# Streaming encoder layer: frame tiles ahead of weights in the first loads, u products by tile as weight blocks arrive, the streams' u later, the last four tiles in halves

## What is computed

```python
h = rms_norm(x, norm_g)
proj = einsum('btd,de->bte', h, w_in)              # 1024 -> 2560
u, g_pool, v_a, v_b, g_conv = split(proj)          # 512 each
pooled = multiscale_pool(u_ext)                    # trailing mean over 2,4,8,16 frames, minus the frame
pooled = (pooled per group @ pool_mix) * pool_scale
pool_out = silu(g_pool) * pooled
v = v_a * sigmoid(v_b)
c = silu(layer_norm(causal_dwconv(v_ext, dw_w, dw_b)))   # 31 taps
conv_out = silu(g_conv) * (c @ pw_w + pw_b)
y = x + concat(pool_out, conv_out) @ w_out
out = rms_norm(y, final_g)
```

## Time and profile before

| what | value |
|---|---|
| runs of the kernel | 282.57, 283.54, 283.54 us, median 283.54 |
| the profiled execution, its time | 284.08 us |
| its span, first to last instruction, slowest core (core 3) | 282.7 us |
| spans of cores 0 to 7 | 280.7, 282.3, 281.2, 282.7, 278.7, 281.8, 278.8, 280.4 us |
| busy share, PE / DVE / ACT / POOL, core 3 | 91% / 64% / 54% / 21% |
| chain that ended last, by engine | PE 64%, ACT 13%, DVE 11%, issue 5%, POOL 3%, DMA 2% |

### The profile page before, as it was taken

One profiled execution on the slowest core, in us unless ns is written; L12 is line 12 of the kernel. 1 busy time (PEld: TensorE's weight loads), 2 busy tenths in 40 slices (PEclk: granted clock), 3 DMA queues, 4 the chain that ended last, 5 costly groups with the idle time before them and its releaser, 6 DMA issues.

```text
span 282.7 us, 4638 instructions; the slowest of 8 cores (278.7 to 282.7 us)
## 1 busy us (share of the span) xinstructions
PE 257.5 (91%) x1768; PEld 140.0 (50%) x1768; DVE 180.0 (64%) x287; ACT 151.8 (54%) x267; POOL 60.2 (21%) x105
## 2 busy tenths in 40 slices
PE   3376999899899999999999899999999999999980
PEld 1175557657444454444566554545444544454430
DVE  1434244455499999999953595357573874767592
ACT  1343734988832459752299726825716634261453
POOL 0129543534500000007100002102202211121232
PEclk9999989999999899999999999999999999999998
DMA  6999999400799463529399029131435532635324
GB/s 132 310 336 340 327 286 332 129 1 2 85 200 193 148 102 95 92 78 205 70 167 165 5 40 326 27 131 74 150 104 196 212 130 106 215 111 211 151 112 184
DMA packets 22952, 44.37 MB, mean 157 GB/s; under 512 B 9649, under 2 KB 13361, under 8 KB 22802
## 3 DMA queue, kind: packets, MB, share of 16 engines
q1 hardware_dynamic: 21154, 38.90, 45.0%
q0 software_dynamic: 1488, 4.85, 11.0%
q10 hardware_dynamic: 288, 0.33, 0.3%
HBM read 38.00 MB, written 10.93 MB: 173 GB/s over the span
## 4 chain that ended last, share of the span: by engine, by line
PE 64%; ACT 13%; DVE 11%; issue 5%; POOL 3%; DMA 2%; SPq 0%; DVEq 0%; ACTq 0%
PE PS L377 59%; PE PS L381 5%; ACT WT L359 5%; DVE PL L373 3%; ACT HG L428 3%; DMA XA<-xp 2%; DVE HG L373 2%; DVE XR L362 2%; POOL STAT L362 2%; ACT HT L359 2%; DVE PA L362 2%; ACT JUNKB L428 1%; DVE XF L362 1%; ACT LNOT L359 1%; POOL STAT L366 1%
## 5 line engine op out<-in xcount | busy, mean ns | idle before, releaser
L377 PE MATMUL PS<-HT,WIN 128*128 128x512 bf16 (+1 forms) x832 | 149.9, 338 | 4.1 <-ACT HT L359 3.1
L377 PEld LDWEIGHTS PS<-HT,WIN 128*128 128x128 bf16 x832 | 72.3, 101 | 69.5 <-issue 6.5
L366 POOL TENSOR_SCALAR STAT<-STAT 128x1 f32<-128x1 f32 (+2 forms) x34 | 14.1, 414 | 112.9 <-ACT JUNKB L428 71.9
L373 DVE SCALAR_TENSOR_TENSOR HG<-XA,STAT,GB 128x1024 bf16<-128x1024 f32 x16 | 21.9, 1371 | 24.9 <-POOL STAT L362 20.6
L428 ACT ACTIVATE JUNKB<-XR 128x1024 bf16<-128x1024 f32 x13 | 13.8, 1058 | 44.6 <-DVE XR L362 44.6
L359 ACT ACTIVATE WT<-WTAB,PP 128x384 bf16<-128x384 f32 x64 | 33.6, 606 | 0.0
L362 DVE TENSOR_TENSOR XR<-PS,XR 128x512 f32<-128x512 f32 x32 | 22.0, 688 | 17.8 <-PE PS L377 17.8
L377 PE MATMUL PS<-WOUT,PL 128*128 128x512 bf16 x128 | 32.9, 379 | 0.0
L377 PE MATMUL PS<-WOUT,MIXC 128*128 128x512 bf16 x128 | 32.9, 379 | 0.0
L359 ACT ACTIVATE HT<-PS 128x1024 bf16<-128x1024 bf16 x16 | 16.4, 1024 | 17.9 <-PE PS L381 17.7
L377 PEld LDWEIGHTS PS<-WOUT,MIXC 128*128 128x128 bf16 x128 | 12.5, 98 | 15.1
(11 more groups left out here) (107 smaller groups left out, 275.4 us busy)
## 6 DMA issues: line engine op xcount, KB each, us to landing
XA<-xp SPq DMA_DIRECT2D x16, 512.0 KB, 16.0
XR<-xp SPq DMA_DIRECT2D x16, 512.0 KB, 3.6
yp<-XR SPq DMA_DIRECT2D x13, 512.0 KB, 2.8
STG<-w_in SPq DMA_DIRECT2D x12, 512.0 KB, 15.8
vdram<-VST SPq DMA_DIRECT2D x4, 520.0 KB, 5.4
VS<-vdram SPq DMA_DIRECT2D x4, 520.0 KB, 5.8
WIN<-w_in POOLq DMA_DIRECT2D x2, 1024.0 KB, 15.9
WOUT<-w_out POOLq DMA_DIRECT2D x1, 2048.0 KB, 20.2
```

Source lines behind the costliest of these rows:

```text
L366: S.op(eng, lambda e: e.tensor_scalar(out=out, in0=a, scalar1=s1, scalar2=None, op0=op0), reads=reads, writes=writes)
L373: S.op('dve', lambda e: e.scalar_tensor_tensor(out=out, in0=a, scalar=s, in1=b, op0=op0, op1=op1), reads=reads, writes=writes)
L377: S.op('pe', lambda e: e.matmul(out, lhsT=lhsT, rhs=rhs, start=start, stop=stop), reads=reads, writes=writes)
```

## The change

1. First loads. On SP's queue the order of the first 512 KB transfers was x0, w8, w9, x1, w10, w11, x2, x3 (x: tile, w: weight block); it is now x0, x1, w8, w9, x2, w10, x3, w11. All later loads keep their order.
2. The first quarter's u. `pre(1)` stands ahead of `trans(0)`, and `utile` is called in smaller pieces: a block of columns for a tile as soon as block and tile can be there.
3. `v_unit(0, 1)` and `v_unit(0, 2)` each move ahead: the second ahead of `pre(4)`, the third ahead of `trans(4)`.
4. `u_h()` moves from ahead of `pre(14)` to behind `trans(15)`; the three weight loads that POOL issues move behind `pre(15)`.
5. `last_tiles()` takes tiles 12 to 15 instead of 13 to 15. One half of a tile's scaling at a time now stands right behind the next square on ACT; tile 14 is stored in two halves as 15 is. `fin_pend` for tile 11 moves behind the second half of tile 12.

```diff
@@ last_tiles
-            for i, p in enumerate(range(NPH - 3, NPH)):
+            for i, p in enumerate(range(NPH - 4, NPH)):
...
-                    if i == 0 and hf == 0:
+                    if pend_scale:
+                        pend_scale.pop(0)()
+                    if i == 0 and hf == 1:
                         fin_pend()
                     tt(XF[i][:, sl], xr[:, sl], FGB[:, sl], ALU.mult, [pk, 'FGB'], [fk])
                     if hf == 0:
                         ts(STAT[:, sc:sc + 1], STAT[:, sc:sc + 1], EPS_RMS, ALU.add, [ssk], [ssk], eng='pool')
-                        if pend_scale:
-                            pend_scale.pop()()
...
-                def scale(i=i, p=p, rs=rs, rsk=rsk):
-                    for hf in range(2):
...
+                def scale(hf, i=i, p=p, rs=rs, rsk=rsk):
...
+                    if p >= NPH - 2:
+                        S.op('act' if p == NPH - 1 and hf == 0 else 'sp',
+                             lambda e: e.dma_start(out=yp_d[p][:, sl], in_=XF[i][:, sl]),
...
-                pend_scale.append(scale)
-            pend_scale.pop()()
+                pend_scale += [lambda f=scale: f(0), lambda f=scale: f(1)]
+            while pend_scale:
+                pend_scale.pop(0)()
@@ first loads
         load_x(0)
         load(ID32[:], id_d, 'ID32', 'c_id', 'act')
+        load_x(1)
         stage_win(8, 'sp')
         stage_win(9, 'sp')
-        load_x(1)
+        load_x(2)
         stage_win(10, 'sp')
+        load_x(3)
         stage_win(11, 'sp')
-        load_x(2)
-        load_x(3)
@@ first quarter
         pre(0)
         cast_win(8, 'dve')
+        pre(1)
+        trans(0)
         cast_win(9, 'dve')
-        trans(0)
-        pre(1)
-        utile(0, (0, 1))
         cast_win(10, 'dve')
+        utile(0, (0,))
+        trans(1)
+        utile(0, (1,))
+        utile(1, (0, 1))
+        pre(2)
+        utile(0, (2,))
+        utile(1, (2,))
         cast_win(11, 'dve')
-        trans(1)
-        utile(0, (2, 3))
-        utile(1)
-        pre(2)
         pre(3)
         trans(2)
+        utile(0, (3,))
+        utile(1, (3,))
+        utile(2, (0, 1))
         trans(3)
-        utile(2)
+        utile(2, (2, 3))
         utile(3)
@@ v units
         v_unit(0, 0)
+        v_unit(0, 1)
         pre(4)
         pre(5)
         cast_win(3, 'pool')
         cast_win(7, 'pool')
-        v_unit(0, 1)
+        v_unit(0, 2)
         trans(4)
-        v_unit(0, 2)
         trans(5)
@@ middle: out of the place ahead of pre(14)
-        S.op('pool', lambda e: e.dma_start(out=PMW[:], in_=pmw_d), writes=['PMW'], dma='wpm')
-        load_win(12, 16, 'wgp')
-        load_win(16, 20, 'wgc')
-        u_h()
...
         pre(15)
+        S.op('pool', lambda e: e.dma_start(out=PMW[:], in_=pmw_d), writes=['PMW'], dma='wpm')
+        load_win(12, 16, 'wgp')
+        load_win(16, 20, 'wgc')
...
         trans(15)
+        u_h()
         pool_sample()
```

More of the change, by code:

```diff
@@ L807, in last_tiles @@
                 tt(rs, STAT[:, sc:sc + 1], NEGH[:, 0:1], ALU.pow, ['SSL%d' % sc, 'NEGH', 'STAT'], [rsk], eng='pool')
-                def scale(i=i, p=p, rs=rs, rsk=rsk):
-                    for hf in range(2):
-                        sl = slice(hf * 512, hf * 512 + 512)
-                        fk = 'XF%d_%d' % (i, hf)
-                        if p == NPH - 1 and hf == 1:
-                            ts(XF[i][:, sl], XF[i][:, sl], rs, ALU.mult, [fk, rsk], [fk])
-                        else:
-                            act(XF[i][:, sl], XF[i][:, sl], AF.Copy, [fk, rsk], [fk], scale=rs)
-                        if p == NPH - 1:
-                            S.op('sp' if hf else 'act', lambda e, sl=sl: e.dma_start(out=yp_d[p][:, sl], in_=XF[i][:, sl]),
-                                 reads=[fk], writes=['o_yp%d_%d' % (p, hf)], dma='stl%d' % hf)
-                    if p < NPH - 1:
+                def scale(hf, i=i, p=p, rs=rs, rsk=rsk):
+                    sl = slice(hf * 512, hf * 512 + 512)
+                    fk = 'XF%d_%d' % (i, hf)
+                    if p == NPH - 1 and hf == 1:
+                        ts(XF[i][:, sl], XF[i][:, sl], rs, ALU.mult, [fk, rsk], [fk])
+                    else:
+                        act(XF[i][:, sl], XF[i][:, sl], AF.Copy, [fk, rsk], [fk], scale=rs)
+                    if p >= NPH - 2:
+                        S.op('act' if p == NPH - 1 and hf == 0 else 'sp',
+                             lambda e: e.dma_start(out=yp_d[p][:, sl], in_=XF[i][:, sl]),
+                             reads=[fk], writes=['o_yp%d_%d' % (p, hf)], dma='stl%d%d' % (p % 2, hf))
+                    elif hf == 1:
                         S.op('sp', lambda e: e.dma_start(out=yp_d[p], in_=XF[i][:]), reads=['XF%d_0' % i, 'XF%d_1' % i],
                              writes=['o_yp%d' % p], dma='st%d' % (p % 6))
-                pend_scale.append(scale)
-            pend_scale.pop()()
+                pend_scale += [lambda f=scale: f(0), lambda f=scale: f(1)]
+            while pend_scale:
+                pend_scale.pop(0)()
         def fin2(p, rs, rsk):
@@ L867, in build_program @@
         JUNKB = at(0, "JUNKB", (128, 1024), BF16)[0]
-        XF = [at(16384 + 4096 * i, "XF%d" % i, (128, 1024), F32)[0] for i in range(3)]
+        XF = [at(16384 + 4096 * i, "XF%d" % i, (128, 1024), F32)[0] for i in range(4)]
         S.op('pool', lambda e: e.memset(NEGH[:], -0.5), writes=['NEGH'])
@@ L1083, in build_program @@
                 p = 4 * q + pq
-                if p == NPH - 3:
+                if p == NPH - 4:
                     last_tiles()
@@ L1115, in build_program @@
         outs = ['o_ys', 'o_st']
-        outs += ['o_yp15_0', 'o_yp15_1'] + ['o_yp%d' % p for p in range(NPH - 1)]
+        outs += ['o_yp%d_%d' % (p, hf) for p in (NPH - 2, NPH - 1) for hf in range(2)] + ['o_yp%d' % p for p in range(NPH - 2)]
         S.op('sp', None, reads=outs)
```

## The result

| | before | the change |
|---|---|---|
| median of four runs each | 283.49 us | 279.63 us (279.28 to 279.99) |
| the profiled execution, its time | 284.08 us | 279.82 us |
| spans of cores 0 to 7 | see above | 278.0, 278.1, 278.1, 278.0, 277.8, 277.8, 278.8, 278.0 us |

The ratio is 0.9868, with a 95% interval of 0.9848 to 0.9889: 3.7 us faster (3.1 to 4.3), where 3.4 was forecast. A few executions, of whatever kernel, have a die at a lower clock and take 323 to 328 us; the ratios leave them out. The slowest core was core 3 and is now core 6; the cores, which differed by 4.0 us, now differ by 1.0. So the two profiles must be compared core by core. Core 3 is read first, as before.

What follows compares the result with a forecast made beforehand. It took the front as a chain through all engines, the middle as DVE's, the end as a chain over ACT. Gains of 1.6 us at 140 and 1.8 at the end made 3.4: 283.54 to about 280.2 us, range 278.7 to 282.4.

Steps and rivals of the forecast that it cites:

- The front, 3.0 us: First quarter's u: with tiles loaded earlier and products by tile, its products end at 26.35 instead of 29.36, 3.0 us gained.
- the weight blocks ... are hidden: First loads: weight blocks move back at most two places, about 3 us, without making PE wait.
- The wait behind the third v unit, 0.7 us: Behind tiles 4 and 5's transposes: PE idles 0.6 to 0.7 us for the first copy, leaving 2.3 us gain.
- The two scaled tiles have time enough: Tiles 4 and 5 are scaled in time, since the third v unit covers them; no size given.
- US later against the front's shift: Start of `pool_sample`: DVE's step waits for US and comes 1.1 us later against the front's shift; bounds 0 and 1.6.
- The waits of DVE that go: Middle, 115 to 123: DVE's three waits for PE, 0.7 us in all, go; 0.4 counted, bounds 0.2 and 0.7.
- The end, 1.8 us: Last tiles: DVE's 0.45 us lag goes and the last square starts 1.35 us sooner; together 1.8, bounds 0.6 and 1.9.
- The clock, forecast at nothing: Whole kernel: the price of the granted clock is the same before and after, so nothing enters the sum.
- Rival D: Fuller PE lowers the clock to 0.93, from 160 to 250 costing 6.3 us: 286.5 us, slower; chance 0.06.
- Rival A: DVE swallows the front's gain, so nothing arrives at 140; only the end's 1.8 us remains: 281.7 us; chance 0.15.
- B: Rival: the middle follows PE and all the front's gain arrives, 2.7 + 1.8 = 4.5 us: 279.0 us; chance 0.12.
- C: Rival: the end gives little, as ACT's scalings hold squares up or the last store does: 282.2 us; chance 0.12.

Runs made afterwards that it cites:

- e8: The changed kernel with the casts of weight blocks 3 and 7 on DVE instead of POOL: 279.69 us, ratio 0.9866.
- e12: The changed kernel with the middle as before, `u_h()` and POOL's three load issues early: 279.92 us, ratio 0.9867.
- e7: The changed kernel with only the last three tiles (13 to 15) in halves: 280.32 us, ratio 0.9892.
- e2: The kernel before with only the change's order of loads, of tiles against blocks, and of v units: 280.79 us, ratio 0.9901.
- e1: The kernel before with only the end's code (four tiles in halves, one scaling behind each square, `fin_pend()` one half later): 281.37 us, ratio 0.9917.
- e5: The changed kernel with the first eight loads in the order of before: 281.60 us, ratio 0.9935.

## Why the prediction was right, and where it was not

The time, the range (278.7 to 282.4) and the side hold. Term by term:

**The front, 3.0 us: right in size.** The median core gains 2.9 us at the first U copy. On core 3 tile 1's transposes came 1.3 us earlier than forecast (13.20 for 14.5), but only since tile 0 did: from tile 0's transposes it is 3.4 us, where the forecast has 3.1. Then *the step "the weight blocks ... are hidden" failed*: block 11 came late, its cast began at 19.57, and PE waited 0.90 us. The forecast had named a wait for a load in the first 26 us as what would make it wrong; here it did not undo the gain. From tile 0's transposes to the first U copy it was 16.63 us on core 3 and is 14.68, 1.9 us less, where cores 2 and 7 gain 2.9. I had computed block 10's landing and not that of block 11, the eighth load, whose products stand ahead of tile 3's transposes.

**The wait behind the third v unit, 0.7 us: too small.** It is 1.18 us, and for DVE, not for ACT's copy. "The two scaled tiles have time enough" failed: DVE's scaling takes 1.96 us beside POOL's casts, and `e8` brought it to 1.28 and the wait to 0.51. On core 6 the wait is 2.01 us, for ACT had to wait 0.72 us for tile 4's load, and the clock fell behind it (last section). By the interval to the first PLS, 1.35 us were given back, of which 0.17 are not accounted for. So the front is worth 1.5 us on a median core, where I had 2.3.

**The middle: its terms right, its gain not.** US later against the front's shift was forecast at 1.1 us; from `e12` to the change it is 1.02 (49.10 to 50.12). The waits of DVE that go were forecast at 0.4, and are 0.38 (60.05 to 59.67); the wait for tile 14 at 0.4, and its going is worth 0.5. What I did not draw from my own numbers is that two of the moves are of different sign: `u_h` could have stayed. DVE's gain ahead of the pooling, forecast at 1.2 us, is 0.5 at a whole clock (2.9 less 2.37), and 0.9 at the last T, where the forecast has 1.6. One reading was wrong without touching the sum: from 140 to 160 not ACT (18.27) but PE (19.60) is the fullest.

**The end, 1.8 us: 1.68 by the traces.** 1.28 us of it is the square that no longer waits for tile 14's scalings, as forecast (1.35). The other 0.4, the lag of DVE, went as forecast but not for the reason given: "the step of 1024 columns of tile 12 ... is gone, and this lag with it" fell with `e7`, where that step is still there and the lag is not. The earlier trace rows begin at 273.90, and the step's wait of 1.19 us for its root lies at 268.29, ahead of where I had looked.

**The sum came right partly by luck.** The median core, at a whole clock, wins 2.9 in the front and loses 0.33 behind it (248.88 to 249.21): 2.6 us, not 3.4. The times say 3.1 to 4.3. The rest lies in what sets the slowest core. I had read core 3 alone, and 2.2 of its 251.07 us behind the first copy (248.88 on cores 4 to 7) were a low clock. In the changed kernel it was core 6, having started first of all, that lost 2.45 us ahead of the first PLS: 0.83 by the longer wait for tile 5 and the other 1.6 at a low clock. The next core's span is 0.7 us shorter. And the highest first U copy of the eight cores, 28.3 to 29.4 with the old front in three profiles, is 24.8 to 26.2 in eight of the ten with the new one, so that the slowest core gains about 3.5 us there, a part of it by the clock (next paragraph). Less the 0.33 this makes some 3.2, inside the interval.

**The clock, forecast at nothing: it went the other way.** Rival D did not happen: PE is fuller, and in the change the clock is 1.00 on all cores from 90 to 262. But the price of the clock was not the same before and after. The mean granted clock of a core is 0.989 over the 36 executions of the kernel before in the three groups, and 0.993 with the front alone (`e2`); with the new end it is 0.993 under the old front (`e1`) and 0.995 or 0.996 in every kernel with the new order of the work, `e5` with its old loads among them. (Each pair has the same end, where PE has stopped and the clock costs nothing.) As one minus the clock, times the span, that is from 3.0 down to 2.1 us and from 2.1 down to between 1.2 and 1.5: by this estimate the front wins 0.6 to 1.0 us on an average core by the clock, which the sum left out. The 0.93 of the earlier trace rows was no level but a mean: 1.00 up to about 32.8 and 0.81 behind it.

The rule I had weighed (the Trainium skill, "TensorE: Matmul & The Clock Gate", Part 1) would have held the clock at 13/16; the trace of the kernel before has stretches of 0.81, and they end under full load, below.

Rival A is excluded, though it was nearer than the 1.8 us by which the last T comes earlier by the medians of the cores (136.0 to 134.2): half of that is the low clock of cores 0 to 3 before, and 0.9 is the order's; B is excluded by PE's wait of 1.72 us, and C by the 2.50 us on all cores.

## What to carry to other kernels

Moving work into an idle stretch of the fullest engine wins nothing if a nearly as full engine waits for that work: here the PE wait that was filled had been free, and filling it cost 1.15 us. A large change should be tried part by part, and in intervals between two events of the same core, since loads that land up to 2.3 us apart hide a microsecond in the total. And before a lag at the end is explained, it should be followed back on its engine to the last wait, here seven microseconds ahead of the last add.
